# State blocks of an S5 branch: cosine products and the first scan kept in PSUM banks

## The reference

```python
lam = lax.complex(lam_re, lam_im); dt = jnp.exp(log_dt)[:, None]
a_bar = jnp.exp(lam * dt)                                  # 32 groups x 64 complex states
b_bar = ((a_bar - 1.0) / lam)[..., None] * b_c
bu = jnp.einsum('blgp,gnp->blgn', uf, b_bar)               # l = 512 positions
_, states = lax.associative_scan(combine, (a_seq, bu), axis=1)   # s[l] = a_bar * s[l-1] + bu[l]
y = jnp.einsum('blgn,gpn->blgp', states, c_c).real + d_skip * uf
```

## Time and profile before

| | us |
|---|---|
| median of three runs | 1724.87 (1720.63 to 1724.88) |
| profiled execution | 1721.2 |
| its span | 1719.4 |
| busy over the span: TensorE, VectorE, ScalarE, GpSimd | 1650.9 (96%), 1508.3 (88%), 1077.1 (63%), 507.6 (30%) |
| stretch 43.00 to 232.45 (state blocks): TensorE, VectorE, ScalarE, GpSimd busy | 177.95, 177.46, 55.72, 95.03 of 189.45 |

### The profile page before, as it was taken

One profiled execution on the slowest core, in us unless ns is written; L12 is line 12 of the kernel. 1 busy time (PEld: TensorE's weight loads), 2 busy tenths in 40 slices (PEclk: granted clock), 3 DMA queues, 4 the chain that ended last, 5 costly groups with the idle time before them and its releaser, 6 DMA issues.

```text
span 1719.4 us, 22463 instructions
## 1 busy us (share of the span) xinstructions
PE 1650.9 (96%) x7233; PEld 1106.9 (64%) x7233; DVE 1508.3 (88%) x1683; ACT 1077.1 (63%) x1036; POOL 507.6 (30%) x321
## 2 busy tenths in 40 slices
PE   5899899999999899999999999999999999999996
PEld 2334347766676677777777777777777777777763
DVE  5999889765778899999999999999999999999995
ACT  5323234376455677777777777777777777777771
POOL 4855134482524022132221212212131121211210
PEclk9999899999999999999999999999999999999998
DMA  5111112312137899999999999999999999999973
GB/s 176 49 52 49 50 50 99 121 52 103 41 128 277 347 373 355 359 388 364 368 365 369 378 360 370 361 366 376 355 369 361 373 379 357 367 366 376 375 280 107
DMA packets 91902, 464.78 MB, mean 270 GB/s; under 512 B 21289, under 2 KB 21405, under 8 KB 42616
## 3 DMA queue, kind: packets, MB, share of 16 engines
q1 hardware_dynamic: 80240, 441.67, 67.3%
q0 software_dynamic: 9776, 18.41, 4.4%
q10 hardware_dynamic: 1848, 4.24, 0.7%
HBM read 454.15 MB, written 18.53 MB: 275 GB/s over the span
## 4 chain that ended last, share of the span: by engine, by line
PE 85%; DVE 10%; issue 2%; ACT 1%; DMA 1%; POOL 0%; ACTq 0%; DVEq 0%; POOLq 0%
PE ps L1848 20%; PE ps L1850 20%; PE ps L1849 20%; PE ps L1834 3%; PE ps L1548 2%; PE ps L1856 2%; PE ps L1529 2%; PE ps L1543 2%; PE ps L1631 1%; PE ps L1633 1%; PE ps L1632 1%; DVE w_lo L1255 1%; PE ps L1623 1%; PE ps L1537 1%; PE ps L1750 1%
## 5 line engine op out<-in xcount | busy, mean ns | idle before, releaser
L1255 DVE TENSOR_TENSOR w_lo<-raw,w_hi 128x2048 fp32r<-128x2048 f32 x384 | 873.6, 2287 | 73.7 <-ACT w_hi L898 72.6
L898 ACT ACTIVATE w_hi<-raw 128x2048 fp32r<-128x2048 f32 x384 | 737.0, 1919 | 240.1 <-PE ps L1850 239.7
L1848 PE MATMUL ps<-w_hi,x_hi 128*96 128x512 f32 x1024 | 414.0, 404 | 1.2 <-DVE w_lo L1255 1.2
L1850 PE MATMUL ps<-w_lo,x_hi 128*96 128x512 f32 x1024 | 403.0, 394 | 0.0
L1849 PE MATMUL ps<-w_hi,x_lo 128*96 128x512 f32 x1024 | 402.4, 393 | 0.0
L637 POOL DMA_INDIRECT gate_now<-gate_rows,row_now x32 | 79.7, 2490 | 454.6 <-DVE tok_out L1396 439.4
L1848 PEld LDWEIGHTS ps<-w_hi,x_hi 128*96 128x96 f32 x1024 | 168.1, 164 | 69.0 <-DVE w_lo L1255 2.4
L1850 PEld LDWEIGHTS ps<-w_lo,x_hi 128*96 128x96 f32 x1024 | 165.4, 162 | 70.8 <-issue 0.2
L1848 PE MATMUL ps<-w_hi,a_hi 128*96 128x512 f32 x512 | 204.4, 399 | 5.7 <-DVE a_lo L1366 5.7
L1849 PEld LDWEIGHTS ps<-w_hi,x_lo 128*96 128x96 f32 x1024 | 165.8, 162 | 63.6
L1849 PE MATMUL ps<-w_hi,a_lo 128*96 128x512 f32 x512 | 201.6, 394 | 0.0
(11 more groups left out here) (337 smaller groups left out, 2208.0 us busy)
## 6 DMA issues: line engine op xcount, KB each, us to landing
raw<-in_w_up SPq DMA_DIRECT2D x256, 1024.0 KB, 8.1
raw<-in_w_down SPq DMA_DIRECT2D x128, 1024.0 KB, 9.6
ring<-in_w_in SPq DMA_DIRECT2D x9, 2048.0 KB, 7.8
ring<-in_w_glu SPq DMA_DIRECT2D x4, 1024.0 KB, 6.3
ring<-in_w_o SPq DMA_DIRECT2D x2, 2048.0 KB, 12.3
h<-in_x SPq DMA_DIRECT2D x4, 512.0 KB, 5.5
ring<-in_w_attn_proj SPq DMA_DIRECT2D x1, 2048.0 KB, 7.9
h_rows<-h ACTq DMA_DIRECT2D x4, 512.0 KB, 2.7
```

What stands on the lines that cost most here:

```text
L898: s.activation(hi_of(c)[:, :], raw_of(c), ACT.Copy).then_inc(s_hi, 1)
L1255: d.tensor_tensor(lo_of(c)[:, :], raw_of(c), hi_of(c)[:, :], ALU.subtract).then_inc(s_lo, 1)
L1848: mm(o, xh, hi_of(c)[:, col], start=start, stop=False)
L1850: return mm(o, xh, lo_of(c)[:, col], start=False, stop=stop)
```

## The change

In each state block the cosine products go back into the banks `br` and `bi` that they are read from. The sine products stay in SBUF. The sum goes into `ps[4]`, the difference into SBUF; both are made before the banks are released, so `s_bufree` is raised by the sixth instruction. The first scan works in place in `ps[4]`, and the two products of its result read it there. The second scan stays in SBUF. The C products of q = 0, 1, 2 share bank 5, and q = 3 uses bank 4; `ymm(1)` and `ymm(2)` wait until the y step before them has read bank 5.

```diff
+        def y_bank(q):
+            return ps[5] if q < 3 else ps[4]
...
-                step(d.tensor_tensor(m[:, 0, :], br[:, :], c, ALU.mult))
+                re = ps[4]
                 step(d.tensor_tensor(m[:, 1, :], bi[:, :], sn, ALU.mult))
-                step(d.tensor_tensor(m[:, 2, :], bi[:, :], c, ALU.mult))
-                d.tensor_tensor(m[:, 3, :], br[:, :], sn, ALU.mult).then_inc(s_bufree, 1)
+                step(d.tensor_tensor(m[:, 3, :], br[:, :], sn, ALU.mult))
+                step(d.tensor_tensor(br[:, :], br[:, :], c, ALU.mult))
+                step(d.tensor_tensor(bi[:, :], bi[:, :], c, ALU.mult))
+                step(d.tensor_tensor(re[:, :], br[:, :], m[:, 1, :], ALU.add))
+                d.tensor_tensor(m[:, 2, :], bi[:, :], m[:, 3, :], ALU.subtract).then_inc(s_bufree, 1)
                 dve.wait_ge(s_bufree, j + 1)
-                step(d.tensor_tensor(m[:, 0, :], m[:, 0, :], m[:, 1, :], ALU.add))
-                step(d.tensor_tensor(m[:, 2, :], m[:, 2, :], m[:, 3, :], ALU.subtract))
                 decay = spw[:, 2, j:j + 1].to_broadcast([P, SEQ])
-                step(d.tensor_tensor_scan(m[:, 1, :], decay, m[:, 0, :], 0.0, ALU.mult, ALU.add))
+                step(d.tensor_tensor_scan(re[:, :], decay, re[:, :], 0.0, ALU.mult, ALU.add))
                 step(d.tensor_tensor_scan(m[:, 3, :], decay, m[:, 2, :], 0.0, ALU.mult, ALU.add))
...
-                step(d.tensor_tensor(w[:, 0, :], m[:, 1, :], c, ALU.mult))
+                step(d.tensor_tensor(w[:, 0, :], re[:, :], c, ALU.mult))
                 step(d.tensor_tensor(w[:, 1, :], m[:, 3, :], sn, ALU.mult))
-                step(d.tensor_tensor(w[:, 2, :], m[:, 1, :], sn, ALU.mult))
+                step(d.tensor_tensor(w[:, 2, :], re[:, :], sn, ALU.mult))
...
-                d.scalar_tensor_tensor(uT[:, q, :], uT[:, q, :], dskip[:, q:q + 1], ps[5 - q % 2][:, :],
+                d.scalar_tensor_tensor(uT[:, q, :], uT[:, q, :], dskip[:, q:q + 1], y_bank(q)[:, :],
...
-                if q > 1:
-                    pe.wait_ge(s_yfree, q - 1)
+                if 0 < q < 3:
+                    pe.wait_ge(s_yfree, q)
...
-                        ins = mm(ps[5 - q % 2][rows, :], cblk[:, r, j, :], w_st[j % 5][:, k, :], start=k == 0, stop=k == 3)
+                        ins = mm(y_bank(q)[rows, :], cblk[:, r, j, :], w_st[j % 5][:, k, :], start=k == 0, stop=k == 3)
```

## The result

The changed kernel takes 1709.5 us (median of six runs, 1706.1 to 1711.1), the kernel before beside it 1724.2 (six runs, 1719.8 to 1724.9). The ratio is 0.9915, with a 95% interval of 0.9905 to 0.9925: faster by 14.7 us, 13 to 16. The forecast was 1708.5 with a gain of 15.2. The profiled run took 1711.1 us (span 1709.3).

The account below looks back on a forecast made before the run. VectorE, stretched 25.4 us by GpSimd, and TensorE waiting for its bank releases bound the state blocks. The walk's 15.2 us gain gave 1706.0 from 1721.2 or 1709.7 on the median; 1708.5 was named, range 1703 to 1718.

Parts of the forecast that it names:

- What bounds the kernel: State blocks, 43 to 227 us: VectorE and TensorE alternate; GpSimd's phase work stretches VectorE by 25.4 us.
- (a) Operands: State blocks on VectorE: five of eight exposed instructions leave the collision, removing 14.3 us of stretch, leaving 11.1; first scan 1.22.
- Rival 2: GpSimd's stretch moves onto three still-exposed VectorE instructions: whole 25.4 us, 1726.6, chance 0.03; halfway gain 8, 1716, chance 0.07.
- the walk: TensorE and VectorE stepped from block 0 at 43.0 us to index products at 211.6 against 226.8: gain 15.2.
- (b) PSUM outputs: State blocks: 64 VectorE writes to PSUM taken to cost 0 extra each; bounds considered 0.06 and 0.53 us.
- rival 3: VectorE's PSUM writes are slow: break-even 0.27 us each; at 0.53, 9.0 us slower, 1732.7; chance 0.08.
- (c) Late release: B products' banks released by the sixth instruction, 4.35 us into a block, instead of the fourth, 2.90.
- (d) C products: C products sharing bank 5 wait for y steps at 109 and 154 us, due at 141 and 185: no cost.
- The split of the gain: Of the 15.2 us, half waits on TensorE (4.1, 0.5, 3.9), half the clock after them (1.0, 2.4, 1.9, 2.3).
- Rival 1: TensorE's clock falls after the 1.4 us wait before B product 6, costing 4.1 us: gain 11.1, 1712.6; chance 0.14.
- Rival 4: The change works but TensorE was the limit anyway: gain under 5 us; chance 0.02.
- The end: Behind 227 us these engines start every step, no transfer at a fixed time: the 15.2 us lead arrives whole.

Follow-up runs that it names:

- (2): Kernel before with four of GpSimd's five phase instructions per block left out (values differ): 1698.3 us, one run.
- the fourth experiment: Changed kernel with both scans and all four state products back in SBUF: 1712.6 us beside 1723.1 for the kernel before, ratio 0.9940.
- (1): Kernel before, operands unmoved, B banks released by the sixth instruction of a block instead of the fourth: 1724.4 us beside 1723.1, ratio 1.0009.
- 10: Changed kernel with cosine products written to the scan's bank and SBUF, B banks released by the fourth instruction, subtract exposed again: 1704.4 us, ratio 0.9899 to kernel before.
- 11: Changed kernel unaltered, run and profiled again: 1709.5 us, ratio 0.9924 to the kernel before.
- 5: Changed kernel with B product 1 issued one tile later on TensorE: 1707.8 us, ratio 0.9913 to the kernel before.
- 6: Changed kernel with B product 1 one tile later and B product 7 one tile earlier: 1708.5 us, ratio 0.9913 to the kernel before.
- (3): Changed kernel with four of GpSimd's five phase instructions per block left out (values differ): 1704.4 us, one run.
- 8: Kernel before with GpSimd's first two phase instructions done twice in every block: 1727.6 us beside 1721.5, ratio 1.0036.
- (9): Changed kernel with GpSimd's first two phase instructions done twice in every block: 1709.5 us, ratio 0.9930 to the kernel before.

## Why the prediction was right

- **What bounds the kernel** held: without GpSimd's phases the kernel before loses all but 2.5 of its 25.4 us of stretch, and 20 us of the stage (2).
- **(a) Operands.** The first scan out of PSUM is at 1.228 us, the free bound, so the choice of 1.22 was right; the decay as its one SBUF input is harmless. By the Trainium skill (SBUF — State Buffer, "SBUF: two separate sides") outside the two-port modes only an instruction with two SBUF inputs needs the shared ports, and the trace now agrees for scans (1228 ns with one input in PSUM) as well as for products. The mis-sized term is what stays: 6.3 us and not 11.1. I took each instruction's stretch as its own, and the fourth experiment shows that it is not: less exposure means less stretch on what stays exposed. Rival 2 had the sign of this wrong. The missing 4.8 us did little on the path: in the places that TensorE waits for, blocks 0 and 10 took 10.7 and 10.9 us, as in the walk (10.8).
- **(b) PSUM outputs** cost 0.008 us each (699 against 691). The estimate of 0.065 us, worked out from the Trainium skill's access times (Perfetto Trace Analysis, "Optimizing Scalar/DVE Operations"), is not seen, and rival 3 is out.
- **(c) Late release**: right in kind, too cheap in the changed kernel, where I gave it a wait of 1.4 us at B product 6, a harmless one at B product 1 and nothing for the clock. It costs about 1 us in the kernel before (1), 5 in the changed one (10 against 11).
- **(d) C products**: no wait on line 1599 appears in TensorE's rows, as forecast.
- **The walk.** The index products came at 212.1 (forecast 211.6), B product 2 at 82.1 without a wait (81.5), B product 6 at 169.3 after a wait of 1.47 (168.8, 1.4), block 14 after a stall of 2.85 (2.9). The step that failed is B product 1. I had TensorE reach it 1.2 us before its release, from the trace of before, where the two tiles ahead took 15.66 us. In this run they took 14.00, so it was there 1.7 us earlier relative to the start of B product 0 and stood 2.60 us. The release itself came as in the walk, 18.5 us after B product 0 (18.8). But the clock fell behind the longer wait, and 2.89+23.31 us took the place of 1.92+20.9, 3.4 more (1.7 in (11)): a term that the sum has at nothing. A start 2.4 us earlier made up for it in the absolute times, which is luck, and is why 211.6 looks so close: over the stage the gain is 12.3 here and 14.0 in (11), against 15.2.
- **The split of the gain.** The parts named as waits (4.1, 0.5, 3.9) and clock (1.0, 2.4, 1.9, 2.3) add up to 16.1 and not to 15.2. They leave out 0.3 and 0.2 us of new waits, and three of the four clock terms set an instruction's own duration against a start-to-start time. The 15.2 comes from the walk and does not rest on them.
- **Rival 1**, the clock after the wait before B product 6, did not come in the changed kernel: 1.99+7.13 us at a clock of 1.00. It did come in two siblings, with the same 1.47 us of wait (5 and 6: 8.83 us for the tile, at a clock of 0.84 in (5)), and took 1.7 us there, not 4.1. So its absence was in part luck. The mechanism struck in the place I had not named, the wait of 2.60 us.
- **Rival 4**, TensorE the limit anyway, falls short of the gain, but it describes version 10, where TensorE idles 1.6 us in the stage.
- **The end.** By the medians the lead arrives: 14.7 us, and 12.5 beside (11), against 12.3 and 14.0 over the stage. By the two profiles it does not arrive whole: 14.65 and 16.4 us at the index products (2.4 of either from the earlier start) leave 10.1 and 11.2 at the end. "No transfer there starts at a fixed time, so the lead arrives whole" was too simple, and why is open.

## What to carry to other kernels

Where VectorE and GpSimd work side by side, read VectorE's mean times by the place of the operands: if forms with two SBUF inputs are stretched and those with one input in PSUM are not, try to put one operand of each into a free PSUM bank, intermediate results included, and look at the sum of the stretch again after each step, for it does not add up by instruction. Don't pay for it with a later release of a bank that TensorE waits for: version 10 puts one instruction back into the collision and is 5 us faster. And when such a wait remains, price the clock behind it too, and walk both engines from a start that you have seen in more than one run.

## What the runs showed of the hardware

- A VectorE product or sum that writes 512 columns of f32 to PSUM takes 699 ns against 691, whether or not it writes into the bank that it reads; the scan out of and into PSUM 1228 against 1224 (3) in SBUF undisturbed.
- The collision costs both sides. Single VectorE products take up to 1.76 us in place of 0.69 even in the changed kernel (line 1137 at 163.02), and GpSimd, with the same instructions but one, is busy 12 us less from 43 to 200 us when VectorE's operands leave SBUF.
- TensorE's clock behind a wait, in this stage of all thirteen profiles: after 1.32 us or less nothing was lost, nor after one of 1.82 (8, a wait for ScalarE); after 1.47 nothing in four places and 1.7 us in two; after 1.67 (4) the product and the tile took 2.90 and 9.56, 3.3 us more than at full clock; after 2.0 to 8.3 us between 1.6 and 4 us. The loss is not set by the length of the wait: behind 2.60 us at the same place of the same kernel it was 3.4 and 1.7 us, and behind 8.28 us the product took 3.78, as it had behind 5.29.
- The first two tiles of the stage took 14.0 to 16.6 us from run to run (14.00 after, 15.66 before, 16.63 in (9)), of one kernel or another, with no edit to TensorE's work there.
